# Depthwise convolution of 31 taps: 24 taps on TensorE, the last seven on VectorE

## The reference

```python
def causal_dwconv_2(x, w, b):
    width, ch = w.shape            # width = 31
    y = lax.conv_general_dilated(
        x, w[:, None, :].astype(x.dtype), window_strides=(1,),
        padding=[(width - 1, 0)], dimension_numbers=("NWC", "WIO", "NWC"),
        feature_group_count=ch)
    return y + b.astype(x.dtype)

def conformer_conv(h, w_pw1, b_pw1, w_dw, b_dw, ln_g, ln_b, w_pw2, b_pw2):
    u = h @ w_pw1 + b_pw1
    a, gate = jnp.split(u, 2, axis=-1)
    u = a * jax.nn.sigmoid(gate)
    u = causal_dwconv_2(u, w_dw, b_dw)
    u = jax.nn.silu(layernorm(u, ln_g, ln_b))
    return u @ w_pw2 + b_pw2
```

## Time and profile before

| | us |
|---|---|
| median of 3 runs | 1102.26 (1100.79 to 1106.17) |
| the profiled execution, its own time | 1103.94 |
| its span, first to last instruction | 1102.0 |

### The profile page before, as it was taken

The page is one execution under the profiler, slowest core; times in us unless marked ns, Lnnn a source line. Parts: engine busy times, 40 slices in busy tenths (PEclk is TensorE's granted clock), DMA queues, the critical chain, the costliest instruction groups (busy, mean ns, idle before and its releaser), DMA issues. The chain is left out here.

```text
span 1102.0 us, 22527 instructions
## 1 busy us (share of the span) xinstructions
PE 1061.5 (96%) x8605; PEld 1003.4 (91%) x8605; DVE 733.6 (67%) x1146; ACT 529.1 (48%) x908; POOL 154.8 (14%) x192
## 2 busy tenths in 40 slices
PE   9999889799999999999999999998997999999998
PEld 8999669699999998877999999998985699999998
DVE  6866668565557755424777777777876667776775
ACT  6553555544443445226644444464645555444442
POOL 0060020011123310002001000141014500001000
PEclk9998999899999999999999999999998999999999
DMA  9552205255564553650555555644630045555551
GB/s 347 173 185 84 97 8 184 79 172 180 183 188 154 189 192 119 198 161 21 171 193 189 174 193 185 187 152 140 237 128 20 1 118 171 199 183 188 173 193 57
DMA packets 51043, 169.86 MB, mean 154 GB/s; under 512 B 5665, under 2 KB 10785, under 8 KB 50849
## 3 DMA queue, kind: packets, MB, share of 16 engines
q1 hardware_dynamic: 45216, 163.22, 46.4%
q10 hardware_dynamic: 5760, 5.70, 1.7%
HBM read 162.16 MB, written 1.05 MB: 148 GB/s over the span
## 5 line engine op out<-in xcount | busy, mean ns | idle before, releaser
L1491 DVE TENSOR_TENSOR WL<-WR,WH 128x1024 fp32r<-128x1024 f32 x302 | 378.6, 1268 | 155.4 <-ACT WH L1231 150.1
L849 PE MATMUL acc<-XH,WH 128*128 128x256 f32 x1392 | 403.0, 289 | 7.3 <-DVE VA L1508 2.8
L850 PE MATMUL acc<-XL,WH 128*128 128x256 f32 x1392 | 393.9, 283 | 0.0
L851 PE MATMUL acc<-XH,WL 128*128 128x256 f32 x1392 | 393.7, 283 | 0.0
L1231 ACT ACTIVATE WH<-WR 128x1024 fp32r<-128x1024 f32 x302 | 312.4, 1050 | 130.6 <-PE acc L851 92.1
L849 PEld LDWEIGHTS acc<-XH,WH 128*128 128x128 f32 x1392 | 266.5, 191 | 11.7 <-DVE WL L1491 7.4
L850 PEld LDWEIGHTS acc<-XL,WH 128*128 128x128 f32 x1392 | 266.9, 192 | 0.9
L851 PEld LDWEIGHTS acc<-XH,WL 128*128 128x128 f32 x1392 | 266.7, 192 | 0.0
L849 PE MATMUL big<-UH,WH 128*128 128x256 f32 x608 | 171.6, 282 | 0.6 <-POOL UL L1940 0.5
L850 PE MATMUL big<-UL,WH 128*128 128x256 f32 x608 | 170.8, 281 | 0.0
L851 PE MATMUL big<-UH,WL 128*128 128x256 f32 x608 | 170.5, 280 | 0.0
(11 more groups left out here) (289 smaller groups left out, 1271.9 us busy)
## 6 DMA issues: line engine op xcount, KB each, us to landing
WR<-weights SPq DMA_DIRECT2D x302, 512.0 KB, 3.6
STK<-UP ACTq DMA_DIRECT2D x32, 142.0 KB, 3.9
X<-x_t SPq DMA_DIRECT2D x4, 256.0 KB, 6.3
MEM<-mem_t SPq DMA_DIRECT2D x1, 1024.0 KB, 10.0
result_t<-X SPq DMA_DIRECT2D x4, 256.0 KB, 2.2
CON<-constants SPq DMA_DIRECT2D x1, 880.0 KB, 12.3
CBUF<-KCV ACTq DMA_DIRECT2D x4, 128.0 KB, 5.7
CBUF<-KCV ACTq DMA_DIRECT2D x4, 127.5 KB, 6.2
```

Source lines behind the costliest of these rows:

```text
L849: pe.matmul(out, wh, hi, start=start, stop=False, skip_group_check=True)
L850: pe.matmul(out, wh, lo, start=False, stop=False, skip_group_check=True)
L851: return pe.matmul(out, wl, hi, start=False, stop=stop, skip_group_check=True)
L1491: dve.tensor_tensor(WL[:, cs % SPL], WR[:, cs % RAW], WH[:, cs % SPL].bitcast(F32), ALU.subtract).then_inc(w_low, 1)
```

## The change

The number of stacked passes goes from eight to six: TensorE handles taps 0 to 23. The other seven (`OWN`, taps 24 to 30) are done by VectorE straight from the padded input `UP` into a new tile `CD` of two buffers: one `tensor_scalar` with the weight and the bias, then six `scalar_tensor_tensor`, each waiting for the one before it (`link`). `conv_out` moves from ScalarE to VectorE, where it is one `tensor_tensor` that adds `CD` to the bank. In VectorE's order, group j - 2's first four own taps stand between gate and value of group j, its last three behind the gated product of group j, and `conv_out(j - 3)` behind the gate of group j. After the last group come `conv_out(5)`, the seven taps and `conv_out` of group 6, and those of group 7. The shifted copies and the diagonals become smaller; a memset of the padding goes; the vector of weights gets the seven rows in another layout.

```diff
-QUADS = (CONV_W + 3) // 4
+QUADS = 6
+OWN = CONV_W - 4 * QUADS
@@
-        B = group([("SG", [P, 2, T], F32), ("AT", [P, 2, T], F32), ("UP", [P, UPS, STACKED + 4], F32),
-                   ("CX", [P, KD, T], F32), ("MU", [P, T], F32), ("STK", [P, UPS, 4, STACKED], F32),
+        B = group([("SG", [P, 2, T], F32), ("AT", [P, 2, T], F32), ("UP", [P, UPS, T + CONV_W - 1], F32),
+                   ("CX", [P, KD, T], F32), ("MU", [P, T], F32), ("CD", [P, 2, T], F32), ("STK", [P, UPS, 4, STACKED], F32),
@@ ScalarE
-            def conv_out(j):
-                act.wait_ge(sem("taps_ps"), j + 1)
-                act.activation(CX[:, j], big[:, j % 4, 0:T], ACT.Identity, bias=vec("b_dw", j)).then_inc(sem("cx_whole"), 1)
-
@@
                 stack_shifts(j)
-                if j >= 3:
-                    conv_out(j - 3)
-            for j in range(KD - 3, KD):
-                conv_out(j)
             act.preload_act_table_set("natural_log_exp_and_others")
@@ VectorE
-            dve.memset(UPAD[:, :, CONV_W - 1 + T:], 0.0)
@@
-            for j in range(8):
+            def own_taps(j, first, stop):
+                for n in range(first, stop):
+                    i = 4 * QUADS + n
+                    x, w, o = UPAD[:, j % UPS, i:i + T], vec("w_own", OWN * j + n), CD[:, j % 2]
+                    if n == 0:
+                        dve.wait_ge(sem("up_ready"), j + 1)
+                        link(dve.tensor_scalar(o, x, w, vec("b_dw", j), ALU.mult, ALU.add))
+                    else:
+                        link(dve.scalar_tensor_tensor(o, x, w, o, ALU.mult, ALU.add))
+
+            def conv_out(j):
+                dve.wait_ge(sem("taps_ps"), j + 1)
+                dve.tensor_tensor(CX[:, j], big[:, j % 4, 0:T], CD[:, j % 2], ALU.add).then_inc(sem("cx_whole"), 1)
+
+            for j in range(KD):
                 gate_half(j)
+                if j >= 3:
+                    conv_out(j - 3)
+                if j >= 2:
+                    own_taps(j - 2, 0, 4)
                 value_half(j)
                 gated(j)
+                if j >= 2:
+                    own_taps(j - 2, 4, OWN)
+            conv_out(KD - 3)
+            for j in (KD - 2, KD - 1):
+                own_taps(j, 0, OWN)
+                conv_out(j)
```

More of the change, by code:

```diff
@@ L51 @@
            ("mem_g", 8), ("ff_g", 8), ("final_g", 8), ("mix2_g", 16), ("ffn2_g", 16), ("b_pw1", 16),
-           ("w_dw", 8 * 4 * QUADS), ("b_dw", 8), ("ln_g", 8), ("ln_b", 8), ("b_pw2", 8),
+           ("w_dw", 8 * 4 * QUADS), ("w_own", 8 * OWN), ("b_dw", 8), ("ln_g", 8), ("ln_b", 8), ("b_pw2", 8),
            ("q_g", 1), ("kc_g", 1), ("ks_g", 1), ("kw_g", 1), ("fconv", 2 * UP_TILES * 4),
@@ L166, in program @@
         OS = QT
-        B = group([("SG", [P, 2, T], F32), ("AT", [P, 2, T], F32), ("UP", [P, UPS, STACKED + 4], F32),
-                   ("CX", [P, KD, T], F32), ("MU", [P, T], F32), ("STK", [P, UPS, 4, STACKED], F32),
+        B = group([("SG", [P, 2, T], F32), ("AT", [P, 2, T], F32), ("UP", [P, UPS, T + CONV_W - 1], F32),
+                   ("CX", [P, KD, T], F32), ("MU", [P, T], F32), ("CD", [P, 2, T], F32), ("STK", [P, UPS, 4, STACKED], F32),
                    ("DG", [P, KD, 4 * QUADS, 32], F32)])
-        SG, AT, UPAD, CX, MU, STK, DG = (B[n] for n in ("SG", "AT", "UP", "CX", "MU", "STK", "DG"))
+        SG, AT, UPAD, CX, MU, CD, STK, DG = (B[n] for n in ("SG", "AT", "UP", "CX", "MU", "CD", "STK", "DG"))
         C = group([("GU", [P, 2, T], F32), ("UH", [P, 2, T], F32R), ("UL", [P, 2, T], F32R),
@@ L2070, in stacked @@
     def stacked(w):
-        w = np.concatenate([w, np.zeros((4 * QUADS - CONV_W, D), w.dtype)]).reshape(QUADS, 4, 8, 4, 32)
+        w = w[:4 * QUADS].reshape(QUADS, 4, 8, 4, 32)
         return w.transpose(4, 1, 2, 3, 0).reshape(P, -1)
@@ L2088 @@
         "b_pw1": _features(a["conv_b_pw1_2"][0][gate_then_a], 16),
-        "w_dw": stacked(a["conv_w_dw_2"][0]), "b_dw": _features(a["conv_b_dw_2"][0], 8),
+        "w_dw": stacked(a["conv_w_dw_2"][0]), "w_own": taps(a["conv_w_dw_2"][0][4 * QUADS:], 8), "b_dw": _features(a["conv_b_dw_2"][0], 8),
         "ln_g": _features(a["conv_ln_g_2"][0], 8), "ln_b": _features(a["conv_ln_b_2"][0], 8),
```

## The result

The changed kernel takes 1096.6 us in the median of ten runs (1094.2 to 1099.1), the kernel before 1102.3 us in ten runs beside it (1100.6 to 1106.2). The ratio is 0.994, with a 95% interval of 0.9928 to 0.9952: faster by 5.7 us. The forecast was 1105.5 us, between 1099.0 and 1110.5, with 0.04 on faster by over 0.5%. It was wrong in sign.

What follows compares the result with a forecast made beforehand. PE bounds the steady stretch now; after the change the ACT-DVE loop of 9.39 us and a late tail would. The mean 3.2 us later, added to the 1102.3 us median, gave 1105.5 us, range 1099.0 to 1110.5.

Steps and rivals of the forecast that it cites:

- What PE loses: Convolution taps on PE: two of eight passes go, taps take 2.69 us a group, 0.90 less; at most 7.2 us gained.
- What DVE gets: DVE, per group: seven linked own taps 3.57 us at 0.52 a link, conv_out 0.37, together 3.94, against 5.93 idle.
- the rival by which a link costs nothing: DVE's own taps: 0.40 instead of 0.52 us each, loop about 8.9 us, PE keeps the pace, 1097.3 us; chance 0.03.
- The loop: ACT's WH to DVE and back, pointwise stage: grows 2.18 to 9.39 us against PE's 9.07, so PE waits for its bank.
- The end of the stage: After group 7's AT at 489.87: PE idles some 6 us, last taps partly at half clock, mean 3.2 us later.
- PE is slowed beyond the last taps: Rival: low clock over sums over features, sums of squares and idle passes, 5.5 to 11 us in all, 1110; chance 0.19.
- What lies beside: Outside the stage: chain to pw2 unchanged; smaller diagonals, copies, one memset less, shorter weight vector together -0.3 to 0.3 us.

Runs made afterwards that it cites:

- the pad: Changed kernel plus an unused tile of 8 floats in front of the feed-forward tiles, UH and UL again 32 bytes off a multiple of 64: 1104.35 us, ratio 1.0006.
- before with 56 floats: Kernel before plus an unused tile of 56 floats in front of the feed-forward tiles, convolution unchanged: 1098.94 us, ratio 0.9952.
- Before with 8 floats: Kernel before plus an unused tile of 8 floats in front of the feed-forward tiles, convolution unchanged: 1109.17 us, ratio 1.0046.

## Why the prediction was wrong

- *What PE loses* (2.69 us for the taps): 2.73. Right.
- *What DVE gets*: six linked instructions in 489.38 to 492.50, 0.52 us each; the rival by which a link costs nothing fell. `conv_out` took 0.34, not 0.37. Right.
- *The loop* (9.39 us): 9.33 to 9.41, and 9.80 once, in the group before which the four DMA issues took 3.35 us. Value tiles waited for their bank, most of them for 0.2 us and not the half that was forecast. Right, and the edit that takes the taps out of the loop shows it as the cause.
- *The end of the stage*: `AT` of group 7 was forecast 67.84 us behind the first `SG` and came after 67.80. The last copies landed 0.6 us earlier than I assumed (`UP` to taps 5.8 us, not 6.4; the stage's DMAs landed after 3.5 us in the median instead of 3.9), PE idled 5.2 us, the clock fell and the taps took 4.6. The mean came 2.2 us late where I had said 3.2. Right in kind, 1.0 us too large.
- *PE is slowed beyond the last taps*: from the mean to `pw2` are 9.73 us in both profiles. It did not happen here.
- *What lies beside*: this step failed, twice. I wrote that "smaller copies, one memset less and the shorter weight vector are nothing: bounds -0.3 to 0.3 us together". The shorter weight vector moved the feed-forward operands by 32 bytes, and that was worth 7 us (7.3 by the two ratios, 1.0006 with the pad and 0.994 without; 7.7 by the distances). I costed what each edit executes and not where it puts things. And the diagonals, a "fraction of a microsecond", were worth 1.1: I had looked at who waits for GpSimd's product and not at what DVE does while GpSimd runs; a `WL` of 2.79 us beside one of 1.22 stood in the trace of before.

By these terms: +2.2 for the stage, -1.1 for the diagonals, -7.7 for the address make -6.6 us; measured are -5.7 in the median and -7.8 between the two profiled spans. Of the 6.28 us behind the mean, 1056 matmuls on `UH` and `UL` explain 4.5. The remaining 1.8 is not settled. The stretches at the lower clock behind the mean lie elsewhere and have other lengths in every execution: 13.7 us in the profile before, 7.5 in the one after. With the distances on `UH` and `UL` brought to those of before, the stretch behind the mean is 600.2 us at 7.5 us of low clock (the changed kernel), 601.9 at 13.7 (before) and 604.0 at 20.5 (before with 56 floats). That is about 0.3 us for each us of low clock, an estimate, and would be these executions' clock and not the change. Before with 8 floats doesn't fit it, with 604.1 at 14.3, so the source stays open.

## What to carry to other kernels

A change that resizes any tile in front of others moves all the others; before reading its time as its own, hold the addresses with a pad, or compare the distance between matmuls in a stretch that it does not touch. When work is given to an engine with idle time, find the loop that passes through that engine and put the work outside it: here the same work was worth 8 us more in one place than in the other. And where one engine's instruction holds another's, as here 2.79 us for 1.22, ask for each instruction that shrinks who had been held by it.

## What the runs showed of the hardware

- The distance between float32r matmuls of 256 columns at full clock was 113.3 to 120.0 ns by the SBUF start of the streamed operand against that of the weights, with the instruction stream unchanged: 6% of PE's time in loops that are bound by PE. The Trainium skill ("SBUF — State Buffer", SBUF: two separate sides) says that PE never waits on anyone at SBUF. That sentence is about contention between engines and names no effect of a start address; the runs with pads show one, and none of them shows what PE waits for.
- With all streamed operands 64 bytes below, PE kept 113.3 or 117.8 ns for a whole loop and changed between loops of one execution. Open is what chooses. With mixed distances the long loops kept one pace, but shorter stretches had either.
- A GpSimd instruction with SBUF inputs held DVE's `tensor_tensor` for 1.57 us of an overlap of 1.71: 2.79 us for 1.22.
- Four DMA issues on ACT mostly took 2.5 to 2.9 us, but up to 4.0 now and then and 4.8 once. In the profile with the 4.8, a loop through ACT, the stage was 2 us longer.
